# mLSTM and sparse attention: VectorE operations behind ScalarE queued one step later, denominators and reciprocals taken for two halves at once

## The reference, cut to what matters

```
def mlstm step(carry, inp):                  # the stabilised recurrence, per head
    D = b[t] - b[s] + log_i[s]               # masked to s <= t
    m_t = max(b + m, D.max(-1))
    s = (q @ k^T) * exp(D - m_t)
    num = s @ v + exp(inter - m_t) * (q @ C)
    den = s.sum(-1) + exp(inter - m_t) * (q @ n)
    den = maximum(abs(den), exp(-m_t))
    h = num / den
...
hm = hm * rsqrt(mean(hm * hm) + EPS)

def dsa_attention(q, k, v, iq, ik, iw, rel_bias):
    score = sum_h iw * relu(iq . ik)         # causal; the top 64 keys of each query are kept
    logits = q . k_sel * dh**-0.5 + bias     # -inf outside the selection
    probs = softmax(logits)
    return probs @ v_sel
ha = ha * silu(a_z)
h = h + concatenate([hm, ha]) @ w_out
```

## Time and profile before

| What | us |
|---|---|
| time, median of 3 runs (lowest to highest) | 882.55 (880.82 to 882.99) |
| time of the profiled execution | 882.83 |
| its span, first to last instruction | 881.0 |
| mLSTM stage (first L1712 to last L1731) | 81.4 to 121.0 |
| sparse attention stage (first L1396 to last L1425) | 138.9 to 197.7 |

### The profile page before, as it was taken

How to read it: one execution, slowest core, us unless ns; L and a number is a source line. 1 busy time by engine, 2 the same in 40 slices (tenths; PEclk the granted TensorE clock), 3 DMA queues, 4 the chain that set the end, 5 groups by cost and what they waited for, 6 DMA issues and landing times. The chain is left out here.

```text
span 881.0 us, 14633 instructions
## 1 busy us (share of the span) xinstructions
PE 856.0 (97%) x5810; PEld 754.6 (86%) x5810; DVE 668.0 (76%) x1096; ACT 458.7 (52%) x737; POOL 66.2 (8%) x61
## 2 busy tenths in 40 slices
PE   9999989999999999999999999999999999999996
PEld 9989978767876888699999999679987899999995
DVE  6698798869977996799757857796777876556567
ACT  5564555454556645475454545265564854454450
POOL 1100001000001120011210100110000111001011
PEclk9999999999999999999999999999999999999999
DMA  9856576556965870799866897379617986645501
GB/s 344 298 178 200 191 245 226 191 157 206 337 238 206 276 272 1 304 371 374 288 221 218 290 342 251 118 242 351 226 50 277 330 294 203 210 153 196 187 1 48
DMA packets 56916, 200.67 MB, mean 228 GB/s; under 512 B 6600, under 2 KB 7936, under 8 KB 56848
## 3 DMA queue, kind: packets, MB, share of 16 engines
q1 hardware_dynamic: 55808, 196.50, 63.6%
q0 software_dynamic: 1040, 3.24, 1.2%
HBM read 198.57 MB, written 1.08 MB: 227 GB/s over the span
## 5 line engine op out<-in xcount | busy, mean ns | idle before, releaser
L1230 PE MATMUL ps<-XT,wsp 128*128 128x256 f32 x760 | 215.5, 283 | 2.2 <-DVE wsp L1471 1.3
L1231 PE MATMUL ps<-XT,wsp 128*128 128x256 f32 x760 | 212.5, 280 | 0.0
L1232 PE MATMUL ps<-XT,wsp 128*128 128x256 f32 x760 | 212.3, 279 | 0.0
L1471 DVE TENSOR_TENSOR wsp<-ring,wsp 128x1024 fp32r<-128x1024 f32 x140 | 173.5, 1248 | 7.5 <-ACT wsp L2047 7.3
L2047 ACT CAST wsp<-ring 128x1024 fp32r<-128x1024 f32 x140 | 145.5, 1046 | 61.6 <-PE ps L1232 52.8
L1230 PEld LDWEIGHTS ps<-XT,wsp 128*128 128x128 f32 x760 | 142.9, 188 | 5.9 <-issue 2.9
L1231 PEld LDWEIGHTS ps<-XT,wsp 128*128 128x128 f32 x760 | 142.8, 188 | 0.5
L1232 PEld LDWEIGHTS ps<-XT,wsp 128*128 128x128 f32 x760 | 142.7, 188 | 0.0
L1230 PE MATMUL ps<-wsp,ra 128*128 128x512 f32 (+1 forms) x256 | 97.6, 381 | 2.5 <-DVE ra L1508 1.1
L1232 PE MATMUL ps<-wsp,ra 128*128 128x512 f32 (+1 forms) x256 | 96.9, 379 | 0.0
L1231 PE MATMUL ps<-wsp,ra 128*128 128x512 f32 (+1 forms) x256 | 96.8, 378 | 0.0
(11 more groups left out here) (278 smaller groups left out, 1538.6 us busy)
## 6 DMA issues: line engine op xcount, KB each, us to landing
arena<-in_mod_w SPq DMA_DIRECT2D x48, 512.0 KB, 6.1
ring<-in_mod_w SPq DMA_DIRECT2D x44, 512.0 KB, 4.8
ring<-in_ffn_a SPq DMA_DIRECT2D x28, 512.0 KB, 5.0
ring<-in_ffn_b SPq DMA_DIRECT2D x28, 512.0 KB, 5.0
arena<-in_ffn_o SPq DMA_DIRECT2D x22, 512.0 KB, 4.7
ring<-in_ffn_o SPq DMA_DIRECT2D x22, 512.0 KB, 4.8
arena<-in_ffn_a SPq DMA_DIRECT2D x16, 512.0 KB, 5.4
arena<-in_ffn_b SPq DMA_DIRECT2D x16, 512.0 KB, 4.8
```

The source lines that it names most:

```text
L1230: pe.matmul(o, l[0], r[0], start=start, stop=False)
L1231: pe.matmul(o, l[0], r[1], start=False, stop=False)
L1232: return pe.matmul(o, l[1], r[0], start=False, stop=stop)
L1471: ve.tensor_tensor(w[:, 1024:1024 + n], raw[slot[0]][:, 0:n], w[:, 0:n].bitcast(f32), SUB).then_inc(*done("V", "lo", u, also=[("raw", *slo ...
```

## The change

In the mLSTM the second VectorE operation of `ml_s` becomes a step of its own, `ml_x`, that is queued one task step later: `ml_x(h, 0)` behind `ml_s(h, 1)`, and `ml_x(h, 1)` behind `ml_s(h+1, 0)` and ahead of `ml_o(h)`. The two halves of `ml_o` are queued together; ScalarE takes the absolute value of each denominator from PSUM, then VectorE takes the maximum and the reciprocal of both halves at once, with one instruction each. ScalarE's scaling and squaring become the step `ml_h`, behind both. In the sparse attention the normalisations of two pairs stand together, `norm2`, at the end of the even steps: one reciprocal for both, then two scalings. The last subtraction of `fin_dsa` becomes `fin_lo`, at the end of the same task step. No buffer is added. The numbering of the turning buffers and banks comes out as before.

```
--- before.py
+++ after.py
@@ -33,7 +33,7 @@
 SIDE = 14
 
 
-MLSTM = ("ml_ac", "ml_em", "ml_e", "ml_d", "ml_h", "ml_sq", "ml_ms")
+MLSTM = ("ml_ac", "ml_em", "ml_e", "ml_d", "ml_a", "ml_h", "ml_sq", "ml_ms")
 TABLES = ("ang", "posf", "tab", "tab_k", "tab_r", "tab_c", "tab_sin", "dist", "dist_d")
 
 
@@ -580,7 +580,15 @@
         add("ml_cols", b, prior("bank", b))
         bank.put(b[0])
         yield
-        held = {}
+        held, late_x = {}, []
+
+        def ml_x():
+            h, j, b, s, b0 = late_x.pop(0)
+            add("ml_x", h, j, b, s, b0)
+            if j:
+                bank.put(b0[0])
+                bank.put(b[0])
+
         for h in range(5):
             bs = []
             for j in range(2):
@@ -589,18 +597,23 @@
                     bs.append(b)
                     add("ml_s", h, j, b, prior("bank", b), s, prior("pb", s), bs[0])
                     held.setdefault(h, []).append(s)
+                if late_x:
+                    ml_x()
+                if h < 4:
+                    late_x.append((h, j, b, s, bs[0]))
                 if h and j == 0:
-                    es = held.pop(h - 1)
+                    es, os = held.pop(h - 1), []
                     for t in range(2):
-                        b, s = bank.get(), pt.get()
-                        add("ml_o", h - 1, t, b, prior("bank", b), es, s, prior("pt", s))
-                        bank.put(b[0])
+                        os.append(bank.get())
+                        add("ml_o", h - 1, t, os[t], prior("bank", os[t]), es)
+                    for t in range(2):
+                        s = pt.get()
+                        add("ml_h", h - 1, t, os[t], s, prior("pt", s))
+                        bank.put(os[t][0])
                         pt.put(s[0])
                     for s in es:
                         pb.put(s[0])
                 yield
-            for b in bs:
-                bank.put(b[0])
 
     W.finish(gts)
     lstm = W.beside(mlstm(), LSTM_PACE)
@@ -675,14 +688,25 @@
                 ps[i] = pb.get()
                 add("sc", "dsa", i, bs[i], None, ps[i], prior("pb", ps[i]))
                 bank.put(bs[i][0])
-            if 0 <= i - 1 < n:
-                add("norm", "dsa", i - 1, ps[i - 1])
+            if 1 < i <= n and i % 2 == 0:
+                add("norm2", i - 2, ps[i - 2], ps[i - 1])
+            if fins:
+                fin_lo()
             yield
+        while fins:
+            fin_lo()
+
+    fins = []
+
+    def fin_lo():
+        k, s = fins.pop(0)
+        add("fin_lo", k, s)
+        wk.put(s[0])
 
     def fin_dsa(k, b):
         s = wk.get()
         add("fin_dsa", k, b, s, prior("wk", s))
-        wk.put(s[0])
+        fins.append((k, s))
 
     proj_b("u", 8, "w_az", 0, 4, lambda j, b: add("ev_az", j, b))
     gone.update(lent)
@@ -1379,7 +1403,7 @@
                     pe.matmul(ps[b[0]][:, 256:256 + n], qkT[:, 4 + h, j * 128:(j + 1) * 128], qkT[:, h, j * 128:256],
                               start=True, stop=True).then_inc(*done("P", "fill", *b))
                 elif kind == "ml_o":
-                    h, t, b, before, es, s, _ = a
+                    h, t, b, before, es = a
                     for j in range(t + 1):
                         for e in new("P", ("ml_e", h, j, 2), ("mv", j, h // 2), ("one", 0), ("one", 1), before):
                             pe.wait_ge(*e)
@@ -1712,23 +1736,25 @@
                     ve.scalar_tensor_tensor(o, ps[b0[0]][:, j * 128:256], acol[:, j * 4 + h:j * 4 + h + 1],
                                             C("cmT", 0, n), ADD, ADD).then_inc(
                         *done("V", "ml_e", h, j, 0, also=[("bank", *b0)] if j else []))
+                elif kind == "ml_x":
+                    h, j, b, s, b0 = a
+                    n = 256 - 128 * j
+                    o = pb[s[0]][:, 0:n]
                     for e in new("V", ("ml_e", h, j, 1)):
                         ve.wait_ge(*e)
                     ve.scalar_tensor_tensor(o, ps[b[0]][:, 256:256 + n], 0.25 * 128.0 ** -0.5, o, MUL, MUL).then_inc(
                         *done("V", "ml_e", h, j, 2, also=[("bank", *b)] if j else []))
                 elif kind == "ml_o":
-                    h, t, b = a[0:3]
-                    o = rdn[:, t * 4 + h:t * 4 + h + 1]
-                    for e in new("V", ("ml_o", h, t), ("ml_em",)):
-                        ve.wait_ge(*e)
-                    ve.tensor_scalar(o, ps[b[0]][:, 256:257], -1.0, None, MUL).then_inc(*done("V", "ml_d", h, t, 0))
-                    for e in new("V", ("ml_d", h, t, 0)):
-                        ve.wait_ge(*e)
-                    ve.scalar_tensor_tensor(o, ps[b[0]][:, 256:257], em[:, t * 4 + h:t * 4 + h + 1], o, MAX,
-                                            MAX).then_inc(*done("V", "ml_d", h, t, 1))
-                    for e in new("V", ("ml_d", h, t, 1)):
-                        ve.wait_ge(*e)
-                    ve.reciprocal(o, o).then_inc(*done("V", "ml_d", h, t, 2))
+                    h, t = a[0:2]
+                    if t == 0:
+                        continue
+                    o, m_ = (grid(x, 2)[:, :, h] for x in (rdn, em))
+                    for e in new("V", ("ml_a", h, 1), ("ml_em",)):
+                        ve.wait_ge(*e)
+                    ve.tensor_tensor(o, o, m_, MAX).then_inc(*done("V", "ml_d", h, 0))
+                    for e in new("V", ("ml_d", h, 0)):
+                        ve.wait_ge(*e)
+                    ve.reciprocal(o, o).then_inc(*done("V", "ml_d", h, 1))
                 elif kind == "ev_az":
                     j, b = a
                     o = azT[:, j:j + 2, :]
@@ -1768,6 +1794,18 @@
                     for e in new("V", ("norm", task, i, 0)):
                         ve.wait_ge(*e)
                     ve.tensor_scalar(p, p, smx[:, i:i + 1], None, MUL).then_inc(*done("V", "norm", task, i, 1))
+                elif kind == "norm2":
+                    i, *s = a
+                    n = 128 * (of("dsa", i)[1] + 1)
+                    for e in new("V", ("exp", "dsa", i + 1)):
+                        ve.wait_ge(*e)
+                    ve.reciprocal(smx[:, i:i + 2], smx[:, i:i + 2]).then_inc(*done("V", "norm", "dsa", i, 0))
+                    for j in range(2):
+                        p = pb[s[j][0]][:, 0:n]
+                        for e in new("V", ("norm", "dsa", i, 0)):
+                            ve.wait_ge(*e)
+                        ve.tensor_scalar(p, p, smx[:, i + j:i + j + 1], None, MUL).then_inc(
+                            *done("V", "norm", "dsa", i + j, 1))
                 elif kind == "fin_dsa":
                     k, b, s, before = a
                     f = wk[s[0]][:, 0:256]
@@ -1775,6 +1813,9 @@
                         ve.wait_ge(*e)
                     ve.scalar_tensor_tensor(f, ps[b[0]][:, 0:256], 0.5, azT[:, k, :], MUL, MUL).then_inc(
                         *done("V", "fin_f", k, also=[("bank", *b)]))
+                elif kind == "fin_lo":
+                    k, s = a
+                    f = wk[s[0]][:, 0:256]
                     for e in new("V", ("fin_hi", k)):
                         ve.wait_ge(*e)
                     ve.tensor_tensor(MX[1][8 + k], f, MX[0][8 + k].bitcast(f32), SUB).then_inc(
@@ -2180,10 +2221,16 @@
                         ac.wait_ge(*e)
                     ac.activation(o, o, ACT.Exp).then_inc(*done("A", "ml_e", h, j, 1))
                 elif kind == "ml_o":
-                    h, t, b, _, _, s, before = a
+                    h, t, b = a[0:3]
+                    for e in new("A", ("ml_o", h, t)):
+                        ac.wait_ge(*e)
+                    ac.activation(rdn[:, t * 4 + h:t * 4 + h + 1], ps[b[0]][:, 256:257], ACT.Abs).then_inc(
+                        *done("A", "ml_a", h, t))
+                elif kind == "ml_h":
+                    h, t, b, s, before = a
                     i = t * 4 + h
                     o = hm[:, i, :]
-                    for e in new("A", ("ml_d", h, t, 2)):
+                    for e in new("A", ("ml_d", h, 1)):
                         ac.wait_ge(*e)
                     ac.activation(o, ps[b[0]][:, 0:256], ACT.Copy, scale=rdn[:, i:i + 1]).then_inc(
                         *done("A", "ml_h", h, t, also=[("bank", *b)]))
```

## The result

The changed kernel takes 891.89 us in the median (889.74 to 893.01, 4 runs) against 882.52 us (4 runs): the ratio is 1.0107, with an interval of 1.0083 to 1.0131. It is 9.4 us slower. The direction and the places were forecast, the size was not: 5.3 us were forecast, and 891.89 lies above the range.

What follows compares the result with a forecast made beforehand. The prediction took TensorE to be the bound almost everywhere, VectorE costing only where TensorE waits for it. 882.55 + 2.5 (mLSTM) + 2.75 (sparse attention) = 887.8 us; range for 8 in 10: 884.3 to 889.8.

Steps and rivals of the forecast that it cites:

- the lateness there: mLSTM, last head: TensorE's last product waits for the moved multiplication and goes on 3.9 us later than before.
- The old stalls, 1.35 and 1.4: mLSTM: TensorE's waits at 115.89 (last head's product) and 123.42 (weight block's low part), both forecast to go.
- the stalls at pairs 2, 8 and 14: Sparse attention: the transposes wait for the scaling moved one step later, by 0.8, 3.4 and 0.75 us.
- the old stalls were absorbed: Sparse attention after pair 8: the two old waits, for `gated` and for L1508, vanish because TensorE is late, -2.2 us.
- TensorE goes on at 119.75: mLSTM, last head: `ml_x(3, 1)` starts at 119.4, takes 0.29, and TensorE resumes at 119.75 instead of 115.89.
- Rival A: Both stages: VectorE's queue is the bound, all four old stalls go, 877.6 us; chance 0.10.
- B: Only the mLSTM costs, since VectorE is in step at pair 8: 885.2 us; chance 0.09.
- C: Both stages: old and new stalls cancel, nothing to be measured, 882.5 us; chance 0.07.
- D: mLSTM: the absolute value brings ScalarE table loads, 1.28 us each, 889.5 us; chance 0.04.

Runs made afterwards that it cites:

- filled kernel: The changed kernel plus 32 extra identity matmuls on TensorE, ahead of the last mLSTM product and pair 8's transposes: 888.77 us, ratio 1.0071.
- mlstm_only: The changed kernel with the sparse attention back in its old order, so only the mLSTM part of the change: 886.88 us, ratio 1.0053.
- den_only: The changed kernel with both multiplications directly in their own step and the old attention, so only the denominators changed: 881.25 us, ratio 0.9979.
- late_product: The changed kernel with half 1's multiplication back, no pairing, the product one half step later and half 0's bank released behind its last reader: 878.44 us, ratio 0.9951.
- half1_back: The changed kernel with only the second half's multiplication back in its own step, behind the first half's: 885.92 us, ratio 1.0033.
- dsa_pair8_apart: The kernel before plus the attention part of the change, but pairs 8 and 9 normalised each in its old place: 882.10 us, ratio 0.9995.

## Why the prediction was wrong

The prediction's places were right. The product is held at heads 1, 2 and 3, by 1.3, 0.4 and 3.4 us (waits of 1.18, 0.26 and 3.24 in the trace and 0.16 for the overlap, as in the prediction), the last head setting the sum; the lateness there was forecast as 3.9 and is 4.15. The old stalls, 1.35 and 1.4, are gone. In the attention the stalls at pairs 2, 8 and 14 were forecast as 0.8, 3.4 and 0.75 and are 0.8, 3.8 and 0.95; VectorE was 0.4 us later at pair 8 than taken: pairs 6 and 7 normalised together put the next masking back, with it ScalarE, and the gates' first operation waits 0.86 us for ScalarE (0.50 before). Between 172.75 and 181.72 the old stalls were absorbed for 2.4 (forecast 2.2). In the filled kernel, which has these terms and no fall of the clock in these stages, they come to 5.8 us instead of 5.25; it ran at 888.77, inside the range.

The step that failed is "TensorE goes on at 119.75": the prediction let TensorE go on at the pace it had before. It took a stall to cost its own length. It left out that TensorE comes back from a long one at the lower clock. By the difference of the two columns this cost 2.8 us behind the last head (5.6 - 2.75), which is still 2.8 at 150.68. The stall of pair 8 takes 0.2 of it back (9.9 - 7.3 = 2.6), and behind it the clock costs 1.6 more (11.5 - 7.3 = 4.2). So 5.8 + 4.2 = 10.0 us in the trace, 9.4 in the medians. The size of this term is not fixed: in mlstm_only a stall of the same length (3.24 us in both traces) cost 1.3 us and not 2.8, and the mean clock of the changed kernel's four runs goes from 0.990 (893.01 us) to 0.994 (889.74 us). The trace of before gave no price for it in these two stages: its stalls, at most 1.44 us by the bracket, were followed by a clock of 1.00 in the earlier trace rows. But a stretch at the lower clock stood elsewhere in it, behind a stall of 1.57 us (last section), and the mean clock of 0.996 was there to be asked about. The Trainium skill (TensorE: Matmul & The Clock Gate, HAM oscillation) describes it: a TensorE that is kept waiting is given half its clock and pays for that when work comes. The trace agrees: 3.24 us of waiting, then a granted clock of 0.50 in 120 to 125 us. It would have moved the sum, and was not weighed.

Rival A fell as forecast: the late multiplication ended 4 us behind its old place, so no lead was kept. VectorE got 3.9 us less to do and the kernel lost 9.4: what counted was the distance between VectorE and TensorE in the list, not VectorE's load. The rule of the Trainium skill (Perfetto Trace Analysis, Identifying the Most-Contended Engine), the most occupied engine first, does not agree with the change as made; with den_only and late_product, where nothing is held, it does. B and C did not happen, since pair 8 was not in step; D did not, since no table was loaded.

## What to carry to other kernels

Moving an operation back in its engine's queue, to hide a wait of 0.4 us, moves it behind everything queued between, here 3.8 us of other work. It is free where its engine still gets to the new place before the reader starts, as with half 0 here, or where the reader is moved back as well, as in late_product; before moving it, compare the time at which the reader starts with the time at which the engine gets to the new place, not with the order in the source. A stall of a few microseconds on TensorE should be priced with the lower clock behind it. The two lines that put half 1 back ahead of its reader took the ratio from 1.0107 to 1.0033.

## What the runs showed of the hardware

The fall of the clock is not tied to the length of a stall alone. Between 325 and 340 us two traces have the same idle time (TensorE busy for 3.38 of 5 us in the window that holds it). In the kernel before the clock fell there, in the run with the attention part alone it did not:

```profile
325.00:330.00 5.00, 3.38 (x17) 2.79 (x16) 4.16 (x17) 2.94 (x13) 1.88 (x2) 0.80 0.26 93
330.00:335.00 5.00, 5.00 (x28) 4.22 (x28) 3.17 (x11) 2.02 (x8) 0.00 (x0) 0.86 0.01 3
```

```profile
330.00:335.00 5.00, 3.38 (x23) 2.84 (x23) 4.21 (x19) 3.08 (x13) 1.56 (x1) 1.00 0.27 93
335.00:340.00 5.00, 5.00 (x30) 4.29 (x29) 4.30 (x16) 2.56 (x11) 0.00 (x0) 1.00 0.01 3
```

The longest idle stretch of TensorE in the 7 us ahead of the fall in the kernel before was this one:

```profile
327.09 0.33 PE L1415 MATMUL ps<-cst,pb 128*128 128x128 f32 x1 [1.57 <-DVE pb L1770]
```

It is hardly longer than the 1.44 us at 181.72, behind which the clock stayed at 1.00, and the run without the fall idles the same 1.57 us at this place. So a short stall can be followed by the lower clock as well, and a stall of 3.24 us had 1.3 us of cost behind it in one run and 2.8 in another.

By TensorE's records the run without the fall gained 1.7 us on the kernel before in this place, and so did two other runs without it (half1_back and dsa_pair8_apart). The spread between runs of one kernel goes with it. Of the 21 runs of the kernel before that den_only was compared with, the three with a mean clock of 0.998 took 880.80 to 881.42 us, the twelve with 0.996 or 0.997 took 881.86 to 883.23, and the six with 0.994 took 884.01 to 884.47. That the falls make the whole spread was not tried, but the two go together, so a difference of 1 to 2 us between two kernels is better read at equal mean clock. What decides about the fall stays open. The extra products of the filled kernel were simple ones, 28 records in 3.29 us, of the identity with itself; they were enough to keep the clock.
